# First MLP's second halves as seven block products, weight sums of both MLPs by DMAs within device memory

## What is computed

```python
def sq_relu_mlp(x, w_in, w_out):
    return jnp.square(jax.nn.relu(x @ w_in)) @ w_out

for layer in range(DEPTH):                     # DEPTH = 2
    hn = rms_norm(h, norm_mix_pre[layer])
    m = mixer_ab(...) if layer % 2 == 0 else mixer_ret(...)
    h = h + rms_norm(m, norm_mix_post[layer])
    f = sq_relu_mlp(rms_norm(h, norm_ffn_pre[layer]), ffn_w_in[layer], ffn_w_out[layer])
    h = h + rms_norm(f, norm_ffn_post[layer])
```

## Time and profile before

| | us |
|---|---|
| median of 3 runs | 1478.39 (1477.74 to 1479.36) |
| span of the profiled execution, first to last instruction | 1476.8 |
| PE busy in it | 1436.1 (97%) |
| DVE, ACT, POOL busy | 921.3 (62%), 538.7 (36%), 87.2 (6%) |

### The profile page before, as it was taken

One profiled execution on the slowest core, in us unless ns is written; L12 is line 12 of the kernel. 1 busy time (PEld: TensorE's weight loads), 2 busy tenths in 40 slices (PEclk: granted clock), 3 DMA queues, 4 the chain that ended last, 5 costly groups with the idle time before them and its releaser, 6 DMA issues.

```text
span 1476.8 us, 22066 instructions
## 1 busy us (share of the span) xinstructions
PE 1436.1 (97%) x9650; PEld 1183.2 (80%) x9650; DVE 921.3 (62%) x1200; ACT 538.7 (36%) x632; POOL 87.2 (6%) x89
## 2 busy tenths in 40 slices
PE   9999999998999999998999999999998999999997
PEld 6778777776888888887888888888887788888786
DVE  7768676667655565554665445355447776868654
ACT  7455454533312221223343332332434433433322
POOL 0000000012010100001200000000003000000000
PEclk9999999998999999999899999999998999999999
DMA  5211111101573644631212222222130352434332
GB/s 187 73 36 59 50 59 45 59 30 35 209 270 141 229 175 175 235 110 62 86 58 88 83 86 86 83 89 86 58 114 29 123 191 86 171 115 165 134 112 59
DMA packets 30623, 160.21 MB, mean 108 GB/s; under 512 B 2816, under 2 KB 6912, under 8 KB 15552
## 3 DMA queue, kind: packets, MB, share of 16 engines
q1 hardware_dynamic: 23456, 130.73, 24.4%
q0 software_dynamic: 7072, 28.08, 5.1%
HBM read 144.12 MB, written 14.68 MB: 108 GB/s over the span
## 4 chain that ended last, share of the span: by engine, by line
PE 89%; DVE 6%; ACT 2%; issue 1%; DMA 1%; POOL 1%; DVEq 0%; POOLq 0%
PE bank L388 20%; PE bank L394 20%; PE bank L391 20%; PE bank L691 2%; PE bank L694 2%; PE bank L695 2%; PE bank L1684 2%; PE bank L1681 2%; PE bank L1678 2%; PE bank L996 2%; PE bank L402 1%; PE bank L1003 1%; DVE WL L346 1%; PE bank L593 1%; PE bank L589 1%
## 5 line engine op out<-in xcount | busy, mean ns | idle before, releaser
L388 PE MATMUL bank<-XH,WH 128*128 128x512 f32 x944 | 379.2, 402 | 16.1 <-DVE XL L481 12.6
L394 PE MATMUL bank<-XH,WL 128*128 128x512 f32 x944 | 371.6, 394 | 0.0
L391 PE MATMUL bank<-XL,WH 128*128 128x512 f32 x944 | 371.6, 394 | 0.0
L346 DVE TENSOR_TENSOR WL<-raw,WH 128x2048 fp32r<-128x2048 f32 (+1 forms) x99 | 222.2, 2246 | 148.1 <-ACT WH L340 148.1
L340 ACT ACTIVATE WH<-raw 128x2048 fp32r<-128x2048 f32 (+1 forms) x99 | 185.3, 1873 | 195.5 <-DMA raw<-weights 195.3
L388 PEld LDWEIGHTS bank<-XH,WH 128*128 128x128 f32 x944 | 179.8, 190 | 60.3 <-issue 20.8
L394 PEld LDWEIGHTS bank<-XH,WL 128*128 128x128 f32 x944 | 179.6, 190 | 38.7
L391 PEld LDWEIGHTS bank<-XL,WH 128*128 128x128 f32 x944 | 179.7, 190 | 38.0 <-issue 1.9
L847 ACT ACTIVATE AH<-relu 128x512 fp32r<-128x512 f32 (+1 forms) x64 | 37.9, 592 | 209.1 <-DVE relu L876 209.1
L388 PE MATMUL bank<-AH,WH 128*128 128x512 f32 x256 | 99.7, 389 | 0.0
L394 PE MATMUL bank<-AH,WL 128*128 128x512 f32 x256 | 99.6, 389 | 0.0
(11 more groups left out here) (360 smaller groups left out, 2339.8 us busy)
## 6 DMA issues: line engine op xcount, KB each, us to landing
raw<-weights SPq DMA_DIRECT2D x104, 1024.0 KB, 4.8
block<-weights POOLq DMA_DIRECT2D x12, 1024.0 KB, 5.5
sums_of_blocks<-block POOLq DMA_DIRECT2D x12, 1024.0 KB, 5.4
raw<-sums_of_blocks SPq DMA_DIRECT2D x12, 1024.0 KB, 4.8
raw<-weights SPq DMA_DIRECT2D x8, 512.0 KB, 4.8
h<-x_fm SPq DMA_DIRECT2D x4, 512.0 KB, 7.9
out_tm<-h SPq DMA_DIRECT2D x8, 256.0 KB, 2.6
rc<-ret_const POOLq DMA_DIRECT2D x1, 1536.0 KB, 7.4
```

Source lines behind the costliest of these rows:

```text
L346: nc.vector.tensor_tensor(WL[i][:, :n], raw[i][:, :n], WH[i][:, :n], ALU.subtract).then_inc(S("w_lo"), 1)
L388: mm = pe.matmul(bank[b][:], wh, xh, start=(k == 0), stop=False)
L391: mm = pe.matmul(bank[b][:], wh, xl, start=False, stop=False)
L394: mm = pe.matmul(bank[b][:], wl, xh, start=False, stop=(k == len(xs) - 1))
```

## The change

1. Quarters 0 to 2 of **MLP 0** get the seven block products too, by a new function `seven_by_feature_pe`. It keeps features on partitions: the weights are stationary (128x128), and the moving operand is the 256 early or late tokens (or a sum of the two). A block product has 2 banks x 2 tiles of 128 outputs x 4 row blocks x 3 matmuls = 48 matmuls of 256 columns; a bank of 512 columns holds two tiles of outputs. The quarter's first half, its activation sums and the chunk order are as in MLP 1. A quarter has 11 chunks and not 8.
2. **The weight sums** of both MLPs (six quarters, g = 0 to 5) are made by POOL's DMAs from device memory to device memory, with no buffer in the core and no DVE work: 8 transfers of 1 MB for each quarter, half of them copies (L797, L799 of the new kernel), half of them transfers that add to what stands at the destination (L801). Each waits for the one before it (`sums_moved`).
3. **Their places** in POOL's queue: six after the two additions of each pair of the mixer (24 for MLP 0), six after the two sums of each retention head (24 for MLP 1). SP waits for the 8 of a quarter before that quarter's first weight chunk of the second half.
4. The signs of the sums are other ones, since a transfer can only add: two of DVE's four steps are now SCALAR_TENSOR_TENSOR.

```diff
+        def seven_by_feature_pe(pe, use, c, q, done):
             for i, banks in enumerate(SEVEN_BANKS):
...
+                    for o in range(2):
+                        to, j = bank[b][:, o * HALF:(o + 1) * HALF], 2 * n + o
+                        for k, (xh, xl) in enumerate(blocks_of(slice(0, HALF))[i]):
+                            if j == 0:
+                                block_ready(pe, i, k, q, done)
+                            wh, wl = wtile(ci, k, j * P, T)
+                            mm = pe.matmul(to, wh, xh, start=(k == 0 and o == 0 and not ADDED[i]), stop=False, skip_group_check=True)
...
+                            pe.matmul(to, wh, xl, start=False, stop=False, skip_group_check=True)
+                            mm = pe.matmul(to, wl, xh, start=False, stop=(k == 3), skip_group_check=True)
...
-            nc.vector.tensor_tensor(S_both[:, 0, :], a21, a22, ALU.add).then_inc(S("s_step"), 1)
+            nc.vector.tensor_tensor(S_both[:, 0, :], a22, a21, ALU.subtract).then_inc(S("s_step"), 1)
...
-            nc.vector.tensor_tensor(S_both[:, 1, :], S_both[:, 0, :], a11, ALU.subtract).then_inc(S("s_step"), 1)
+            nc.vector.scalar_tensor_tensor(S_both[:, 1, :], S_both[:, 0, :], -1.0, a11, ALU.mult, ALU.subtract).then_inc(S("s_step"), 1)
...
-            nc.vector.tensor_tensor(S_both[:, 3, :], a12, S_both[:, 1, :], ALU.subtract).then_inc(S("s_step"), 1)
+            nc.vector.scalar_tensor_tensor(S_both[:, 3, :], a12, -1.0, S_both[:, 1, :], ALU.mult, ALU.subtract).then_inc(S("s_step"), 1)
...
+        WEIGHT_SUMS = tuple((g, to, k) for g in range(2 * SEVEN) for to, k in ((0, 0), (0, 2), (2, 2), (2, 3), (3, None), (3, 0), (1, None), (1, 1)))
+
+        def weight_sum_step(pool, n):
+            g, to, k = WEIGHT_SUMS[n]
+            if n:
+                pool.wait_ge(S("sums_moved"), 16 * n)
+            at, to_sum = STORED[g // SEVEN] + 8 * (g % SEVEN) + 4, sums_of_blocks[g, to]
+            if k is None:
+                pool.dma_start(to_sum, sums_of_blocks[g, 2 if to == 3 else 3]).then_inc(S("sums_moved"), 16)
+            elif n % 8 in (0, 2):
+                pool.dma_start(to_sum, weights[at + k]).then_inc(S("sums_moved"), 16)
+            else:
+                pool.dma_start(to_sum, weights[at + k], accum_op=ALU.add, max_dma_last_dim=4 * CHUNK).then_inc(S("sums_moved"), 16)
...
-                for j in range(0, 8 if layer else 16, 2):
+                for j in range(0, 8 if layer or q < SEVEN else 16, 2):
...
+                elif q < SEVEN:
+                    seven_by_feature_pe(pe, use, c, q, done)
...
-                    if not layer and q < SEVEN and j in (9, 11, 13, 15):
-                        weight_sums_dve(dve, 4 * q + j // 2 - 4)
...
             nc.gpsimd.tensor_tensor(chunked(W[4]), chunked(W[4]), table(K_EYE2), ALU.add).then_inc(S("e1"), 1)
+            for n in range(6 * p, 6 * p + 6):
+                weight_sum_step(pool, n)
...
-                if c == FFN1_CHUNK:
-                    sync.wait_ge(S("sums_stored"), 16 * SEVEN * PIECES)
+                for g in range(2 * SEVEN):
+                    if c == FFN_AT[g // SEVEN][g % SEVEN] + 4:
+                        sync.wait_ge(S("sums_moved"), 16 * 8 * (g + 1))
...
                         nc.gpsimd.tensor_tensor(sum_a, sum_a, ysq[:, 0, :], ALU.add).then_inc(S("ysq_summed"), 1)
+                        for n in range(6 * hd, 6 * hd + 6):
+                            weight_sum_step(pool, 8 * SEVEN + n)
```

More of the change, by code:

```diff
@@ L46 @@
 FFN1_CHUNK = RET_CHUNK0 + 8 * RET_HEADS
-SEVEN = 3
-FFN1_AT = [FFN1_CHUNK + 11 * q for q in range(SEVEN + 1)]
-ALL_CHUNKS = FFN1_AT[SEVEN] + 8
+FFN_AT = [[at + 11 * q for q in range(QUARTERS)] for at in (FFN0_CHUNK, FFN1_CHUNK)]
+ALL_CHUNKS = FFN_AT[1][SEVEN] + 8
+STORED = (FFN0_CHUNK, FFN0_CHUNK + 8 * QUARTERS + 8 * RET_HEADS)
 HALF = T // 2
-PIECES = CHUNK // T
 V_NORM = 0
@@ L235, in trunk_kernel @@
         S_both = nc.alloc_sbuf_tensor_at("S_both", [P, 4, HALF], F32, offset=ffn.at - 4 * D)
-        blocks_at = ffn.at - 4 * D - 16 * 2 * T
-        block = [nc.alloc_sbuf_tensor_at(f"block{i}", [P, 4, T], F32, offset=blocks_at + i * 16 * T) for i in range(2)]
         uT = nc.alloc_sbuf_tensor_at("uT", [P, TT, D], F32, offset=start)
@@ L655, in out_by_token_dve, with blocks_of @@
                 stored(TT - 1)
-        def blocks_of(q, t):
-            early, late = slice(t * P, (t + 1) * P), slice(HALF + t * P, HALF + (t + 1) * P)
+        def blocks_of(early):
+            late = slice(HALF + early.start, HALF + early.stop)
             def summed(i):
@@ L684, in seven_pe @@
                         pe.wait_ge(S(f"acc_free{b}"), u - 1)
[L685 to L689 removed]
+                    for k, (xh, xl) in enumerate(blocks_of(slice(t * P, (t + 1) * P))[i]):
+                        if t == 0:
+                            block_ready(pe, i, k, SEVEN + q, done)
                         wh, wl = (w[ci % RING][:, k * T:(k + 1) * T] for w in (WH, WL))
@@ L728, in seven_dve, with activation_sums @@
                     for tokens, outputs, sign in ADDENDS[i]:
-                        to = fT[:, 2 * tokens + t, outputs * T:(outputs + 1) * T]
-                        last = added.get((tokens, outputs, t))
-                        added[tokens, outputs, t] = b, u
-                        if last:
-                            dve.wait_ge(S(f"acc_free{last[0]}"), last[1])
-                        if not last:
-                            ins = nc.vector.tensor_scalar(to, bank[b][:], float(sign), None, ALU.mult)
-                        else:
-                            ins = nc.vector.tensor_tensor(to, to, bank[b][:], ALU.add if sign > 0 else ALU.subtract)
+                        if layer:
+                            to, block = fT[:, 2 * tokens + n, outputs * T:(outputs + 1) * T], bank[b][:]
+                        else:
+                            at = 4 * outputs + 2 * n
+                            to = f[:, at:at + 2, tokens * HALF:(tokens + 1) * HALF]
+                            block = bank[b].rearrange("p (o t) -> p o t", o=2)
+                        if not after_added(dve, layer, tokens, outputs, n):
+                            ins = nc.vector.tensor_scalar(to, block, float(sign), None, ALU.mult)
+                        else:
+                            ins = nc.vector.tensor_tensor(to, to, block, ALU.add if sign > 0 else ALU.subtract)
+                        added[layer, tokens, outputs, n] = b, u
                     ins.then_inc(S(f"acc_free{b}"), 1)
-        def activation_sums(dve, q, k):
-            n = 4 * q + k
-            dve.wait_ge(S("a_square"), 8 * QUARTERS + 8 * q + 4 + k + 1)
+        def activation_sums(dve, g, k, done):
+            n = 4 * g + k
+            dve.wait_ge(S("a_square"), done + 4 + k + 1)
             if n:
@@ L868, in ffn_dve @@
                 c = quarter_at(c0, layer, q)
-                for j in range(8 if layer else 16):
+                g, seven = SEVEN * layer + q, q < SEVEN
+                for j in range(8 if layer or seven else 16):
                     b = j % 4
@@ L887, in ffn_dve @@
                         nc.vector.tensor_tensor(AL[:, j, :n], square[:, :n], AH[:, j, :n], ALU.subtract).then_inc(S("a_lo"), 1)
-                        if layer and q < SEVEN and j > 4:
-                            sums_low(dve, q, j - 5)
-                        if layer and q < SEVEN and j >= 4:
-                            activation_sums(dve, q, j - 4)
-                    else:
+                        if seven and j > 4:
+                            sums_low(dve, g, j - 5)
+                        if seven and j >= 4:
+                            activation_sums(dve, g, j - 4, done)
+                    else:
+                        for tokens in range(2):
+                            after_added(dve, layer, tokens, (j - 8) // 4, (j - 8) % 4 // 2)
                         add_to_f(dve, use, b, j - 8, q == 0)
@@ L897, in ffn_dve @@
                         split_lo(dve, c + j // 2 + 2)
-                    if not layer and q < SEVEN and j in (9, 11, 13, 15):
-                        weight_sums_dve(dve, 4 * q + j // 2 - 4)
-                if layer and q < SEVEN:
-                    seven_dve(dve, use, c, q)
+                if seven:
+                    seven_dve(dve, use, c, q, layer)
                 elif layer:
```

132 lines of the change are left out of this document (61 added, 71 removed).

## The result

The changed kernel is **slower**: 1495.05 us (median of 4 runs, 1492.88 to 1501.07) against 1478.07 us of the kernel before beside it (4 runs), a ratio of 1.0124, interval 1.0102 to 1.0146. The forecast was 1470.5 with a range to 1482: a miss in size and in sign.

What follows compares the result with a forecast made beforehand. PE was taken as the bound, busy 97% of the span and never idle in MLP 0. Terms -11.1 + 1.7 + 0.9 + 0.3 + 0.3 = -7.9 us took the span from 1476.8 to 1468.9, time 1470.5 us, range 1466 to 1482.

Steps and rivals of the forecast that it cites:

- the transfers in POOL's queue: Mixer and retention: six transfers in a row fit POOL's free gaps, and chunk loads up to 4.4 us longer are hidden.
- rival 1: End of mixer and retention: POOL comes late by 19.5 and 12.8 us, so +24.4 in sum, 1502.8 us; chance 0.16.
- rival 3: Mixer: transfers hold up weight chunks beyond the hidden 4.4 us, say 9 us for each of three, 1484.3 us; chance 0.08.
- the 11.6 that was named: Mixer: ACT's wait of 7.24 us for chunks growing beyond 11.6 would be the sign of rival 3.
- S: Sum of three copies at 5.5 us and two adding transfers at 11 us, 38.5 us; ends 27 and 65.5.
- PE's pace: MLP 0's second halves: 0.1185 us per 256-column matmul, saving 3.7 us a quarter, 11.1 us in three.
- Rival 2: MLP 0: narrow matmuls take 0.1233 us, saving 6.3 us, sum -3.1, 1475.3 us; chance 0.12.
- The stall at product 1: MLP 0, quarter 0: PE waits 1.7 us for DVE's late weight split, plus 0.9 us if the clock falls.
- half of 1.7: MLP 0, quarter 0, behind the stall: lower clock costs up to 1.7 us more; half, 0.9 us, was taken.
- The DVE steps: Two of four steps become SCALAR_TENSOR_TENSOR: 0.3 us more in MLP 0 and 0.3 us in MLP 1.
- the 9% of rows 8: At 512 columns SCALAR_TENSOR_TENSOR takes 752 ns against 693 for TENSOR_TENSOR; the basis for costing the DVE steps.
- the arithmetic part of the forecast: Whole kernel: -11.1 + 1.7 + 0.9 + 0.3 + 0.3 = -7.9 us, with nothing for the transfers.

Runs made afterwards that it cites:

- experiment 1: Changed kernel without the mixer's 24 transfers; MLP 0's second halves read plain weights instead of sums: 1472.72 us, ratio 0.9957.
- 2: Changed kernel with the mixer's 12 adding transfers turned into plain copies, so 24 copies: 1513.59 us, ratio 1.0232.
- 3: Changed kernel with only one copy and the 12 adding transfers in the mixer, all to one destination: 1511.02 us, ratio 1.0215.
- experiment 5: Changed kernel with its 48 transfers cut in shorter rows, copies 8 KB and adding ones 2 KB: 1498.34 us, ratio 1.0146.
- experiment 6: Changed kernel with the mixer's 24 transfers replaced by 1 MB stores from the core's memory to device memory: 1493.62 us, ratio 1.0098.
- 4: Changed kernel with MLP 0's sum transfers moved: eight behind `y_affine` of pairs 1 to 3, sixteen in MLP 0: 1478.89 us, ratio 1.0003.
- 8: As 7, but quarter 2's last four sum transfers follow at once behind quarter 1's six: 1476.27 us, ratio 0.9988.
- 9: As experiment 1, plus 15 more 1 MB copies in the retention, five behind each of the first three heads' six: 1472.6 us, ratio 0.9973.
- 10: Changed kernel, MLP 0's 24 transfers moved: four from first freed chunk, twelve behind `y_affine`, two at MLP 0's start, six in quarter 1: 1475.91 us, ratio 0.9986.
- 7: Changed kernel, MLP 0's transfers moved: twelve behind `y_affine`, two at MLP 0's start, six in quarter 1, four in quarter 2: 1486.2 us, ratio 1.0052.

## Why the prediction was wrong

**The step that failed** is the paragraph on the transfers in POOL's queue and what it lets through: "These transfers share the DMA engines with the weight chunks." It asked who waits for POOL (rival 1) and who waits for a chunk (rival 3) and took that for all. PE's supply of instructions was not on the list, and its term was nothing. The runs show 22 us in its place (1495.05 against 1472.72 in experiment 1): 15 us of idle time for want of instructions, and 7 of clock. Neither rival was it: POOL waits for ACT where it should have been late, and ACT's wait of 7.24 us is 7.21 in the changed kernel, far from the 11.6 that was named. The wrong sign came from a cause without a case of its own.

**What the pieces are.** They come with copies, adding transfers, short pieces and stores alike (2, 3, 5, 6), and only beside 64- and 128-column matmuls (1, 4, 8, 9, 10). The trace shows what PE waits for. DMA packets of the queue "instruction" in 50 us (packets, MB, share): mixer, 60 to 110 us, then retention, 865 to 915 us, in the kernel before.

```profile
q8 instruction: 8, 0.13, 1.0%
```

```profile
q8 instruction: 2, 0.03, 0.3%
```

The instructions come through the same DMA engines, four times as many packets in the mixer. Over the whole execution the page of the changed kernel counts 80 packets of 16 KB in this queue for 20164 matmuls and weight loads of PE (before: 76 for 19300), one for about 250 of them, so the queue is PE's.

Each idle piece ends behind such a packet. The twelve profiles have 101 pieces of "issue" on PE after 50 us, and every one ends 1.2 to 1.6 us after a packet of this queue has ended; of moments picked at random in the changed kernel's mixer, 5% lie like that. For the piece of 2.88 us, this is the window of 0.1 us in which the packet starts, 75.0 to 75.1 us in the changed kernel, and 72.3 to 72.4 us in the kernel before (the share times 1.6 us is its duration, 0.9 us in both):

```profile
q8 instruction: 1, 0.02, 55.9%
```

```profile
q8 instruction: 1, 0.02, 57.4%
```

In the kernel before PE goes on at the same place without a pause:

```profile
74.14 1.01 PE L977 MATMUL bank<-cst,W 128*128 128x128 f32 x4
75.08 1.15 PE L1003 MATMUL bank<-W,W 64*64 64x64 f32 x32
```

PE reaches that place at 74.14 before and at 74.19 now, but the packet starts 2.7 us later, ends at 76.0, and PE goes on at 77.40. The packets are not slow in themselves: from 55 to 345 us they take 1.04 us on average in both kernels. They start late. Matched with experiment 1 by PE's place in its instructions, the 19 of the mixer's 34 packets that are due while packets of POOL's queue are in flight start 1.6 us late on average, the other 15 at their time. So it is shown that PE runs out of instructions because their packet starts late beside a transfer. What holds the packet back is not shown. The length of the transfer's packets is not it alone: with the short ones of experiment 5 the instruction packets are 1.5 us late too.

The Trainium skill, "SBUF — State Buffer", section "Who interferes with whom", says that DMA never contends with a compute engine. It speaks of the ports of the core's memory, and experiments 8 and 9 agree with it at DMA shares up to 0.75; for an engine as a whole, instructions included, it does not hold here, as the 17.7 us of issue show.

**POOL's transfers.** A copy at 5.5 us was right (5.5 to 5.8), an adding one at 11 too dear (7.9 to 8.6); S is 33.5 us, not 38.5, and fits everywhere, as said.

**PE's pace.** 0.1185 us was a little low. Three matmuls take 0.36 us, each 0.1200; the first and the last of seven steps:

```profile
427.07 0.28 PE L715 MATMUL bank<-AH,WH 128*128 128x256 f32 x1
...
429.59 0.28 PE L715 MATMUL bank<-AH,WH 128*128 128x256 f32 x1
```

A quarter's second half is 40.3 us for the 43.5 before; three save 9.6, not 11.1. Rival 2's 0.1233 was not reached.

**The stall at product 1** was in its place, but has two waits. PE, changed kernel:

```profile
417.55 0.39 PE L715 MATMUL bank<-AH,WH 128*128 128x256 f32 x1 [1.63 <-DVE WL L345]
...
418.60 0.28 PE L719 MATMUL bank<-AH,WL 128*128 128x256 f32 x1
419.60 0.58 PE L715 MATMUL bank<-AH,WH 128*128 128x256 f32 x1 [0.73 <-DVE AL L903]
419.99 0.41 PE L718 MATMUL bank<-AL,WH 128*128 128x256 f32 x1
420.20 0.41 PE L719 MATMUL bank<-AH,WL 128*128 128x256 f32 x1
```

The first is the 1.7 us of the prediction (1.63). The second was not seen: AL of tile 7 stands third behind the late split in DVE's queue, and costs 1.00 - 0.12 = 0.9 us from start to start. Then PE runs at 0.21 us a matmul instead of 0.12, its lower clock level (1.2 GHz), which costs 1.4 us, where half of 1.7 was taken. So the term is 3.9 us and not 2.6. In experiment 1 the clock did not fall behind the same two waits: 9.6 - 1.6 - 0.9 = 7.1 us, and its MLP 0 gains 7.2. In the changed kernel 9.6 - 3.9 = 5.7, and the norm before MLP 0, at a lower clock, takes 0.8 us more, so 4.9 for the 4.5 measured.

**The DVE steps.** The 0.3 us taken in each MLP are nothing: on 256 columns the new instruction is no longer than the old. The third step, before and changed:

```profile
1170.07 0.42 DVE L750 TENSOR_TENSOR S_both<-S_both,first_squared 128x256 f32<-128x256 f32 x1
```

```profile
409.21 0.42 DVE L783 SCALAR_TENSOR_TENSOR S_both<-S_both,first_squared 128x256 f32<-128x256 f32 x1
```

MLP 1's stall did go from 1.82 to 2.05 us, 0.23 more, but that this looks like the 0.3 is luck: over the kernels of the experiments it lies between 1.85 and 2.63.

```profile
1193.27 0.50 PE L688 MATMUL bank<-WH,AH 128*128 128x512 f32 x1 [2.05 <-DVE WL L345]
```

The half throughput that the Trainium skill gives for this instruction ("Vector Engine (DVE) Microarchitecture Reference", section "Points that are easy to get wrong") would have made it 1.6 us more. The trace disagrees, 0.42 us for either; and the 9% of rows 8 does not carry over to 256 columns.

**Retention**: -2.6 us was not forecast. In the 44 us behind the end of MLP 0 the profiled execution of the kernel before has a clock of 0.84, the changed one 0.88, which is some 1.7 of these 2.6 us; the heads follow each other at 101.3 us in both. I count it as no effect of the change, but no run shows that.

So the arithmetic part of the forecast, -7.9, comes to about -5 (1472.72 against 1478.11 in experiment 1), within the range given, and the transfers add 22 that were taken as nothing.

## What to carry to other kernels

Before moving data "for free" in the background, look at what each engine does in that stretch, not only at who waits for data: where PE runs tens of small matmuls in a microsecond, keep megabytes of DMA out, and put them beside wide matmuls. The same 24 transfers cost 22 us at one place and about 4 at another. And where a late instruction of an in-order queue is costed, read the two or three behind it too: the next wait is often for one of them.

## What was not expected of the hardware

- PE idle for want of instructions beside any 1 MB transfers, always until 1.2 to 1.6 us after a packet of its instruction queue: 17.7 us with mixed ones, 21.2 with copies, 20.3 with 13 transfers, 14.7 with short rows, 9.8 with stores, 1.6 to 3.6 without any in those stretches.
- The clock, from 50 us on. In the five kernels with transfers beside small matmuls it was below 1.00 in several stretches of the mixer, in experiments 4, 7 and 9 in one (0.90, 0.90 and 0.86 from 50 to 100 us, with no transfer near), in the kernel before and experiments 1, 8 and 10 in none. In experiment 6 that cost some 18 us beside 7.1 of idle time. So some of it comes without transfers, and it is more with them; what decides is open.
- From issue to landing an adding transfer within device memory takes 8.3 us per megabyte (median of 24), a copy 5.2 to 5.5 in the first 50 us of them and 5.7 to 6.1 over the whole execution, a store from the core's memory 4.4.
